# Other loading order and earlier sums of weights in three down stages of a feed-forward kernel

## The chip, the cores and the metric

The kernel runs on one core of a Trainium2 chip. The metric is the device time of one execution in microseconds (us), as a median of runs. A change of under 0.2% (4.9 us here) counts as no change.

## What is computed

The program is two transformer blocks on 256 rows of width 2048, in float32. Only the second feed-forward matters here:

```python
h = rms_norm(x, norm_mlp_pre[l])
u = jnp.square(jax.nn.relu(h @ w_up[l]))          # 256 x 8192
x = x + rms_norm(u @ w_down[l], norm_mlp_post[l])  # w_down: 8192 x 2048
```

A product in full precision is made of three TensorE products in the type fp32r. Each operand is split into a high part (rounded to fp32r) and a low part (the rest); the products are high x high, high x low and low x high.

## The kernel before

**Passes and stages.** The 8192 hidden columns are done in four passes of 2048. A pass is an up stage of 32 steps and a down stage. The down stages of passes 0, 1 and 2 are the full ones that the title speaks of (`DOWN2_STEPS`, 44 steps, numbered 0 to 43 here); the last pass has another list (`LAST_DOWN2`), and the first feed-forward has a third (`DOWN1_STEPS`). A step multiplies by one 256 x 512 piece of weights.

**Plain steps and sevens.** The down product is cut into column blocks b (0 to 3, 512 columns each) and into eighths j of the 2048 rows of weights that a pass uses (0 to 7, 256 rows each). A plain step (b, j) has 12 matmuls. For some pairs of column blocks and groups of rows, four blocks in a 2 x 2 arrangement are multiplied with seven products instead of eight, as in Strassen's method. Such a seven is the steps (pair, group, k), k from 0 to 6, with 6 matmuls each. Products k = 0, 1, 2 take weights as they are loaded. Products k = 3, 4, 5, 6 take sums of weights (sum 0, 1, 2, 3), which VectorE makes by subtraction at L1808. The order of a full down stage begins: steps 0 to 3 plain (0,4) (0,5) (1,4) (1,5); steps 4 to 10 the seven (0,0); steps 11 and 12 plain (0,6) (0,7); steps 13 to 19 the seven (0,1); steps 20 to 23 plain (1,6) (1,7) (2,4) (2,5). Then two more sevens follow, at steps 24 to 30 and 35 to 41.

**The split of a step.** Before TensorE can do step n, ScalarE writes the high part of its weights to `wh` (L908), and then VectorE writes the low part to `wl` (L1464), four slots each. I call them the high part and the low part of n. Both engines work in program order and are three steps ahead: in the program's place s (the s-th turn of the loop, called `ahead(s)`) they split the weights of step s+3. The high part of n waits until TensorE has finished step n-4, whose slot it takes, and until the load has landed. The low part counts `lo_done` up by one, and TensorE's step waits for that count.

**Sums.** `weight_sums` is called after `ahead(s)` and the other work of place s. `sums_begin` says at which place sum 0 is made; the others follow one place apart. Sum 3 takes the buffer of sum 0, so it waits for the low part of product k = 3. For the seven (0,0) the places are 1, 2, 3 and 4, for the seven (0,1) 11, 12, 13 and 14.

**Loads.** Weights come in loads of 1 MB (512 rows of weights by 512 columns, two steps' worth) into four `raw` slots. SyncE's queue issues them in the order of `DOWN2_LOADS`, whose entries are (b, group of rows); the load number u takes slot u mod 4. In front of each issue the queue waits until the load four places earlier is used up:

```python
def ff2_load(u, w, k, col):
    sp.wait_ge(lo_done, load_done(u - RAW_SLOTS))
    sp.dma_start(raw[u % RAW_SLOTS][:], w[:, k:k + 4, col:col + COLS]).then_inc(raw_in[u % RAW_SLOTS], 16)
```

`load_done` gives the count of low parts after which a load's slot is free. For a load that feeds only plain steps this is the low part of its second step: load (0,2) feeds steps 0 and 1, load (1,2) feeds steps 2 and 3, load (0,3) feeds steps 11 and 12. For the two loads of a seven it is the low part of product k = 4 (k = 5 in the seven (0,1)). By then all four sums have been made; for the loads (0,0) and (1,0) this is step 8's low part, made at place 5.

**VectorE's other work around the change.** In the up stages VectorE also adds, squares and splits the hidden values (L2143, L2147, L2165), and in passes 1 and 2 it folds the products of the last pass into the rows (`combine`, L1830 and L1852).

Of the kernel before, what the change touches and what calls it, by code (L numbers as in the profile page):

```python
# [66 lines left out]
def seven(pair, group):  # L67
    return [(pair, group, k) for k in range(7)]
# [17 lines left out]
for _n in range(2):  # L86
# [4 lines left out]

DOWN2_STEPS = [(0, 4), (0, 5), (1, 4), (1, 5)] + seven(0, 0) + [(0, 6), (0, 7)] + seven(0, 1) + [(1, 6), (1, 7)]
DOWN2_STEPS += [(2, 4), (2, 5)] + seven(1, 0) + [(2, 6), (2, 7), (3, 4), (3, 5)] + seven(1, 1) + [(3, 6), (3, 7)]
DOWN2_LOADS = [(0, 2), (1, 2), (0, 0), (1, 0), (0, 3), (0, 1), (1, 1), (1, 3),
               (2, 2), (2, 0), (3, 0), (2, 3), (3, 2), (2, 1), (3, 1), (3, 3)]

LAST_DOWN2 = [(0, 2), (0, 3), (0, 4), (0, 5), (1, 2), (1, 3)] + seven(0, 0)
# [8 lines left out]
for _p in range(UP2_PASSES):  # L106
# [7 lines left out]
DOWNS = [(S_DOWN1[p], L_DOWN1[p], DOWN1_STEPS, DOWN1_LOADS) for p in range(2)]  # L114
DOWNS += [(S_DOWN2[p], LOADS_BEFORE + 32 * p + 16, DOWN2_STEPS, DOWN2_LOADS) for p in range(UP2_PASSES - 1)]
DOWNS += [(S_DOWN2[-1], LOADS_BEFORE + 32 * (UP2_PASSES - 1) + 16, LAST_DOWN2, LAST_LOADS2)]
SEVENS = [(s0 + n, step[0], step[1]) for s0, _, steps, _ in DOWNS for n, step in enumerate(steps)
          if len(step) == 3 and step[2] == 0]


def sums_begin(steps, pair, group):

    late = steps is DOWN2_STEPS and (pair, group) == (0, 1)
    return steps.index((pair, group, 0)) - (2 if late else 3)


def load_of(step):
# [22 lines left out]
def load_done(u):  # L150

    for s0, first, steps, loads in DOWNS:
        if first <= u < first + len(loads):
            b, group = loads[u - first]
            if (b // 2, group, 0) in steps:
                return s0 + sums_begin(steps, b // 2, group) + 8
            return s0 + steps.index((b, 2 * group + 1)) + 1
    if u >= LOADS_BEFORE:
        p, r = divmod(u - LOADS_BEFORE, 32)
        return S_UP2[p] + 2 * r + 2  # L160
    part = max(p for p in range(3) if p == 0 or u >= L_UP1[p])
    return (S_UP1[part] if part else 0) + 2 * (u - (L_UP1[part] if part else 0)) + 2
# [135 lines left out]
def build(nc, a, out, scratch, scratch_cols, scratch_scales):  # L298
# [6 lines left out]
    def at(name, shape, kb, dt=F32):  # L305
        return nc.alloc_sbuf_tensor_at(name, shape, dt, offset=int(base + kb * KB))
# [50 lines left out]
    w_sum = [at(f"w_sum{i}", [P, 2, COLS], kb) for i, kb in enumerate((192, 196, 201))]  # L357
# [170 lines left out]
    def sums_before(q):  # L528

        return 4 * sum(q >= n + 7 for n, _, _ in SEVENS)  # L530
# [22 lines left out]
    def _(sp):  # L553
# [3 lines left out]
        def weight_load(u, i, src):  # L557

            if u >= RAW_SLOTS:
                sp.wait_ge(lo_done, load_done(u - RAW_SLOTS) + 8 * i)  # L560
            sp.dma_start(raw[u % RAW_SLOTS][:], src).then_inc(raw_in[u % RAW_SLOTS], 16)
# [201 lines left out]
# [4 lines that stand above are left out]
# [688 lines left out]
    def _(dve):  # L1455
# [337 lines left out]
        def weight_sum(down, pair, group, n, w_sum):  # L1793

            s0, first_load, steps, loads = DOWNS[down]
            u = first_load + loads.index((2 * pair, group))
            for v in (u, u + 1):
                dve.wait_ge(raw_in[v % RAW_SLOTS], 16 * (v // RAW_SLOTS + 1))
            (b11, b21), (b12, b22) = ([raw[v % RAW_SLOTS][:, 2 * k:2 * k + 2, :] for k in range(2)] for v in (u, u + 1))
            q = s0 + steps.index((pair, group, 0))  # L1800
            made = sums_before(q)
            if n == 2:
                dve.wait_ge(sem["sum_ok"], made + 1)
            if n == 3:
                dve.wait_ge(sem["sum_ok"], made + 3)
                dve.wait_ge(lo_done, q + 4)
            plus, minus = ((b12, b11), (b22, b12), (b22, w_sum[0][:]), (b21, w_sum[2][:]))[n]
            dve.tensor_tensor(w_sum[n % 3][:], plus, minus, ALU.subtract).then_inc(sem["sum_ok"], 1)  # L1808

        def weight_sums(down, s, w_sum):  # L1810

            s0, _, steps, _ = DOWNS[down]
            for n7, step in enumerate(steps):
                if len(step) == 3 and step[2] == 0:
                    n = s - sums_begin(steps, step[0], step[1])
                    if 0 <= n < 4:
                        weight_sum(down, step[0], step[1], n, w_sum)

        def combine(p, pair, k, to_x=True):

            shared, rows_to = (shared1, x_rows) if to_x else (shared2, y_rows)
            (p1, p5), (p6, p7) = ([shared[pair][h][:, c, :] for c in range(2)] for h in range(2))
            (x11, x12), (x21, x22) = ([rows_to[:, t, (2 * pair + b) * COLS:(2 * pair + b + 1) * COLS]
                                       for b in range(2)] for t in range(NT))

            def put(dst, src, t):

                if to_x:
                    return dve.tensor_tensor(dst, src, dst, ALU.add)
                return dve.scalar_tensor_tensor(dst, src, rstd_sq[:, t:t + 1], dst, ALU.mult, ALU.add)  # L1830

            if k == 0:
                dve.wait_ge(sem["shared_out"], 2 * p + pair + 1 if to_x else folds(p, pair))
                if to_x:
                    dve.wait_ge(sem["rows_added"], 16 * (4 * p + 2 * pair + 2))
                elif p:
                    dve.wait_ge(sem["rows_added"], 16 * added(p, 2 * pair + 1))
                else:
                    dve.wait_ge(row_free, FREE + R_DOWN2[0] + 2 * pair + 2)
                put(x11, p1, 0)  # L1840
            if k == 1:
                chain.link(dve.tensor_tensor(p6, p6, p1, ALU.add))
            if k == 2:
                chain.link(dve.tensor_tensor(p7, p7, p6, ALU.add))
            if k == 3:
                put(x21, p7, 1)
            if k == 4:
                chain.link(dve.tensor_tensor(p7, p7, p5, ALU.add))
            if k == 5:
                put(x22, p7, 1)  # L1850
            if k == 6:
                chain.link(dve.tensor_tensor(p5, p5, p6, ALU.add))  # L1852
            if k == 7:
                put(x12, p5, 0).then_inc(sem["combined"], 1)
# [346 lines left out]
        for p in range(UP2_PASSES):  # L2201
            for r in range(S_UP2[p + 1] - S_UP2[p] if p + 1 < UP2_PASSES else N_STEPS - S_UP2[p]):
# [13 lines left out]
                n = r - 32  # L2216
# [53 lines left out]
    def _(pe):  # L2270
# [151 lines left out]
        def head_stage(j, k, last):  # L2422
# [50 lines left out]
            if j == 3 and k - 1 >= first[0]:  # L2473
                n = k - 1
                kind, h, x, _, _, (vb, vc) = heads[n]
                if outs_before(n):
                    pe.wait_ge(sem["at_osb"], outs_before(n))
                acc = psum[:, O_BANK, 0:SEQ]
                if n < N1:
                    v, count = values(n)  # L2480
                    pe.wait_ge(sem["at_vlo"], count)
                    pe.wait_ge(sem["at_ptlo"], n + 1)
                    for kt in range(NT):
                        p_h, p_l = prob_hi[n % 2][:, kt, :], prob_lo[n % 2][:, kt, :]
                        pe.matmul(acc, v[:, 0, kt, :], p_h, start=kt == 0, stop=False)
                        pe.matmul(acc, v[:, 0, kt, :], p_l, start=False, stop=False)
                        ins = pe.matmul(acc, v[:, 1, kt, :], p_h, start=False, stop=kt == 1)
                    ins.then_inc(sem["at_o"], 1)
                    return
                pe.wait_ge(sem["at_ptsb"], n + 1)  # L2490
                if kind == "slc":
                    pe.matmul(acc, cmp_v[:, h % 4, h // 4, :], cmp_pt[:, h // 4, :], start=True, stop=False)
                for kt in range(NT):
                    q0 = P * kt
                    ins = pe.matmul(acc[:, q0:SEQ], x[:, vb, kt, vc:vc + HD], prob_t[n % 2][:, kt, q0:SEQ],
                                    start=False, stop=kind != "slc" and kt == 1)
                ins.then_inc(sem["at_o"], 1)
# [495 lines left out]
```

## Time and profile before

| | |
|---|---|
| median of 3 runs | 2460.39 us (2460.31 to 2460.43) |
| profiled execution, its own time | 2460.36 us |
| its span, first to last instruction | 2458.6 us |
| TensorE busy | 2446.9 us |
| VectorE busy | 1729.2 us |
| ScalarE busy | 1321.1 us |
| mean over 16 DMA engines | 196 GB/s |

The profiled execution lies 0.03 us under the median and 1.8 us over its span, so a difference in the span can be added to the median as it stands. All times inside the kernel count from the start of the span. A matmul is shown with its full duration, of which the next one overlaps a part; what counts is the distance between starts.

### The profile page before, as it was taken

To read this page: it belongs to the slowest core of one execution; us is meant where nothing else is said; L and a number is where in the kernel's file an instruction comes from. 1 tells how busy PE (TensorE), PEld (TensorE's weight loads), DVE (VectorE), ACT (ScalarE), POOL (GpSimd) and SP (SyncE) were. 2 spreads that over 40 slices of the span, in tenths; PEclk is the share of its full clock that TensorE was granted. 3 is DMA by queue.
4 is the path that set the end of the run, shared out by engine and by line. 5 is a ranking of instruction groups with operands and counts; after the bars stand their busy time and mean duration, and the time that the engine had idled before them with its cause. 6 is when DMAs were issued, how large, how long until landed. Compare 5 with 4: busy or idle time off the path is not lost.

```text
span 2458.6 us, 31658 instructions
## 1 busy us (share of the span) xinstructions
PE 2446.9 (100%) x12392; PEld 2073.4 (84%) x12392; DVE 1729.2 (70%) x2080; ACT 1321.1 (54%) x1690; POOL 67.3 (3%) x91
## 2 busy tenths in 40 slices
PE   9999999999999999999999999999999999999998
PEld 7888888888888888888888788888888888888887
DVE  5756767655678777787875457755668779788676
ACT  6444556445555655565555445444646546556453
POOL 0100100000000000000000000000000000000000
PEclk9999999999999999999999999999999999999999
DMA  9655565655555765567557565555564656756763
GB/s 328 207 192 172 164 173 170 224 187 188 190 188 171 245 200 188 188 205 235 182 199 248 157 206 167 163 171 173 171 196 175 228 189 205 222 168 234 218 211 128
DMA packets 255910, 480.84 MB, mean 196 GB/s; under 512 B 23296, under 2 KB 26752, under 8 KB 255152
## 3 DMA queue, kind: packets, MB, share of 16 engines
q1 hardware_dynamic: 251296, 470.85, 57.4%
q0 software_dynamic: 4352, 8.39, 1.9%
q8 instruction: 74, 1.21, 0.2%
q14 instruction: 44, 0.36, 0.0%
q10 hardware_dynamic: 144, 0.03, 0.0%
HBM read 468.71 MB, written 2.13 MB: 192 GB/s over the span
## 4 chain that ended last, share of the span: by engine, by line
PE 96%; DVE 3%; issue 1%; ACT 0%; DVEq 0%; POOLq 0%; POOL 0%; ACTq 0%
PE psum L2376 21%; PE psum L2285 14%; PE psum L2287 14%; PE psum L2286 14%; PE psum L2384 11%; PE psum L2601 3%; PE psum L2603 3%; PE psum L2602 3%; PE psum L2620 2%; PE psum L2622 2%; PE psum L2621 2%; PE psum L2341 1%; DVE wl L1464 1%; PE psum L2346 1%; DVE w_sum L1808 1%
## 5 line engine op out<-in xcount | busy, mean ns | idle before, releaser
L1464 DVE TENSOR_TENSOR wl<-raw,wh 128x1024 fp32r<-128x1024 f32 x833 | 1014.2, 1225 | 647.8 <-ACT wh L908 641.8
L908 ACT ACTIVATE wh<-raw 128x1024 fp32r<-128x1024 f32 x833 | 873.9, 1058 | 774.4 <-PE psum L2287 319.3
L2285 PE MATMUL psum<-wh,ha 128*128 128x512 f32 x1248 | 499.5, 400 | 0.1
L2287 PE MATMUL psum<-wh,ha 128*128 128x512 f32 x1248 | 487.1, 390 | 0.0
L2286 PE MATMUL psum<-wl,ha 128*128 128x512 f32 x1248 | 486.4, 390 | 0.0
L2376 PE MATMUL psum<-ha,wh 128*128 128x512 f32 x1344 | 313.1, 390 | 0.0
L2376 PEld LDWEIGHTS psum<-ha,wh 128*128 128x128 f32 x1344 | 249.7, 188 | 50.1
L2287 PEld LDWEIGHTS psum<-wh,ha 128*128 128x128 f32 x1248 | 234.2, 188 | 50.8
L2285 PEld LDWEIGHTS psum<-wh,ha 128*128 128x128 f32 x1248 | 234.7, 188 | 47.7 <-issue 2.7
L2286 PEld LDWEIGHTS psum<-wl,ha 128*128 128x128 f32 x1248 | 235.0, 188 | 44.7
L2376 PE MATMUL psum<-hb,wh 128*128 128x512 f32 x896 | 209.1, 390 | 0.0
L2376 PEld LDWEIGHTS psum<-hb,wh 128*128 128x128 f32 x896 | 166.4, 188 | 33.4
L2384 PEld LDWEIGHTS psum<-ha,wl 128*128 128x128 f32 x1344 | 166.8, 192 | 3.3
L2384 PE MATMUL psum<-ha,wl 128*128 128x256 f32 x1344 | 167.8, 283 | 0.0
L2384 PEld LDWEIGHTS psum<-hb,wl 128*128 128x128 f32 x896 | 111.2, 192 | 2.2
L2384 PE MATMUL psum<-hb,wl 128*128 128x256 f32 x896 | 111.9, 283 | 0.0
L908 ACT ACTIVATE wh<-w_sum 128x1024 fp32r<-128x1024 f32 x76 | 80.7, 1062 | 50.6 <-PE psum L2603 28.6
L2601 PE MATMUL psum<-wh,ha 128*128 128x512 f32 x240 | 93.6, 390 | 0.7 <-DVE wl L1464 0.7
L1464 DVE TENSOR_TENSOR wl<-w_sum,wh 128x1024 fp32r<-128x1024 f32 x76 | 90.1, 1220 | 4.7 <-ACT wh L908 4.6
L2603 PE MATMUL psum<-wh,ha 128*128 128x512 f32 x240 | 93.4, 389 | 0.0
L2602 PE MATMUL psum<-wl,ha 128*128 128x512 f32 x240 | 93.4, 389 | 0.0
L2285 PE MATMUL psum<-wh,hb 128*128 128x512 f32 x224 | 87.8, 392 | 0.0
(337 smaller groups left out, 2843.6 us busy)
## 6 DMA issues: line engine op xcount, KB each, us to landing
raw<-in_w_up SPq DMA_DIRECT2D x152, 1024.0 KB, 5.1
raw<-in_w_in SPq DMA_DIRECT2D x116, 1024.0 KB, 5.1
raw<-in_w_down SPq DMA_DIRECT2D x108, 1024.0 KB, 5.1
raw<-in_w_out SPq DMA_DIRECT2D x32, 1024.0 KB, 5.0
raw<-in_w_branch_a SPq DMA_DIRECT2D x8, 1024.0 KB, 5.0
raw<-in_w_branch_b SPq DMA_DIRECT2D x8, 1024.0 KB, 4.9
x_rows<-conv POOLq DMA_DIRECT2D x8, 512.0 KB, 6.7
raw<-in_w_in SPq DMA_DIRECT2D x5, 512.0 KB, 8.0
```

The lines of the kernel that those rows point to most:

```text
L908: act.activation(wh[q % SPLIT_SLOTS][:], src, ACT.Copy).then_inc(hi_done, 1)
L1464: dve.tensor_tensor(wl[q % SPLIT_SLOTS][:], src, wh[q % SPLIT_SLOTS][:].bitcast(F32), ALU.subtract).then_inc(lo_done, 1)
L2285: pe.matmul(acc, hi, wh[s][:, c, :], start=first and c == 0, stop=False)
L2286: pe.matmul(acc, hi, wl[s][:, c, :], start=False, stop=False)
L2287: ins = pe.matmul(acc, lo, wh[s][:, c, :], start=False, stop=last and c == 1)
L2376: ins = pe.matmul(psum[:, 4 * v + d, :], wh[s][:, c, P * d:P * d + P], both, start=(j, n, c) == (0, 0, 0), stop=(j, n, c) == (6, 1, 1))
L2384: ins = pe.matmul(psum[:, 4 * v + d, 0:SEQ], wl[s][:, c, P * d:P * d + P], src[:, 2 * (j + n) + c, 0, :], start=False, stop=False)
L2601: pe.matmul(acc, hi, wh[w][:, c, :], start=first and c == 0, stop=False)
L2602: pe.matmul(acc, hi, wl[w][:, c, :], start=False, stop=False)
L2603: ins = pe.matmul(acc, lo, wh[w][:, c, :], start=False, stop=last and c == 1)
L2620: pe.matmul(acc, hi, wh[w][:, c, :], start=first and c == 0, stop=False)
L2621: pe.matmul(acc, hi, wl[w][:, c, :], start=False, stop=False)
```

## The change

The order of the first four loads of a full down stage becomes (0,0), (1,0), (0,2), (1,2). Sums 0, 1 and 2 of the seven (0,0) are made at the places -4, -3 and -2, which are turns 28, 29 and 30 of the up stage before. Sum 3 of every seven is made at the place of its product k = 0, which is where it was for all but the seven (0,1), whose sum 3 moves from place 14 to place 13, directly behind sum 2. `load_done` is rewritten, and comes to the same counts as before for every load of every seven, so (0,0) and (1,0) are released by step 8's low part still. Sum 0 has one more wait, for the low parts of the seven before.

```diff
-DOWN2_LOADS = [(0, 2), (1, 2), (0, 0), (1, 0), (0, 3), (0, 1), (1, 1), (1, 3),
+DOWN2_LOADS = [(0, 0), (1, 0), (0, 2), (1, 2), (0, 3), (0, 1), (1, 1), (1, 3),
                (2, 2), (2, 0), (3, 0), (2, 3), (3, 2), (2, 1), (3, 1), (3, 3)]
...
 def sums_begin(steps, pair, group):
 
-    late = steps is DOWN2_STEPS and (pair, group) == (0, 1)
-    return steps.index((pair, group, 0)) - (2 if late else 3)
+    ahead = {(0, 0): 8, (0, 1): 2}.get((pair, group), 3) if steps is DOWN2_STEPS else 3
+    return steps.index((pair, group, 0)) - ahead
...
             if (b // 2, group, 0) in steps:
-                return s0 + sums_begin(steps, b // 2, group) + 8
+                return s0 + max(sums_begin(steps, b // 2, group) + 8, steps.index((b // 2, group, 4)) + 1)
...
             made = sums_before(q)
+            if n == 0 and made:
+                dve.wait_ge(lo_done, [s + 7 for s, _, _ in SEVENS if s < q][-1])
             if n == 2:
...
                     n = s - sums_begin(steps, step[0], step[1])
-                    if 0 <= n < 4:
+                    if 0 <= n < 3:
                         weight_sum(down, step[0], step[1], n, w_sum)
+                    if s == n7:
+                        weight_sum(down, step[0], step[1], 3, w_sum)
```

## Rows read from the trace of the kernel before

**Rows 1.** The page: busy us (share of the span) xinstructions

```profile
PE 2446.9 (100%) x12392; PEld 2073.4 (84%) x12392; DVE 1729.2 (70%) x2080; ACT 1321.1 (54%) x1690; POOL 67.3 (3%) x91
```

**Rows 2.** Waits of TensorE: us in total, times, longest us

```profile
PE psum L2620 <- DVE wl L1464: 1.1, 4, 0.4
PE psum L2601 <- DVE wl L1464: 0.7, 3, 0.2
```

**Rows 3.** Timeline of TensorE, pass 0's down stage: start, us, line

```profile
1869.64 0.39 PE L2622 MATMUL psum<-wh,ha 128*128 128x512 f32 x1
1870.27 0.47 PE L2601 MATMUL psum<-wh,ha 128*128 128x512 f32 x1 [0.24 <-DVE wl L1464]
...
1875.81 0.39 PE L2620 MATMUL psum<-wh,ha 128*128 128x512 f32 x1
...
1882.98 0.50 PE L2620 MATMUL psum<-wh,a_hi 128*128 128x512 f32 x1 [0.21 <-DVE wl L1464]
...
1885.88 0.39 PE L2601 MATMUL psum<-wh,ha 128*128 128x512 f32 x1
```

**Rows 4.** Timeline of VectorE, the same stage

```profile
1861.87 1.22 DVE L1464 TENSOR_TENSOR wl<-w_sum,wh 128x1024 fp32r<-128x1024 f32 x1
1863.22 1.22 DVE L1808 TENSOR_TENSOR w_sum<-raw,w_sum 128x1024 f32<-128x1024 f32 x1
1864.37 3.48 DVE L1464 TENSOR_TENSOR wl<-w_sum,wh 128x1024 fp32r<-128x1024 f32 x3
...
1868.91 4.62 DVE L1464 TENSOR_TENSOR wl<-raw,wh 128x1024 fp32r<-128x1024 f32 x4
...
1877.16 1.23 DVE L1464 TENSOR_TENSOR wl<-w_sum,wh 128x1024 fp32r<-128x1024 f32 x1 [0.23 <-ACT wh L908]
1878.30 1.22 DVE L1808 TENSOR_TENSOR w_sum<-raw,w_sum 128x1024 f32<-128x1024 f32 x1
1879.44 1.22 DVE L1464 TENSOR_TENSOR wl<-w_sum,wh 128x1024 fp32r<-128x1024 f32 x1
...
1881.71 2.44 DVE L1464 TENSOR_TENSOR wl<-w_sum,wh 128x1024 fp32r<-128x1024 f32 x2
```

**Rows 5.** Timeline of VectorE, last turns of two up stages

```profile
1844.21 2.36 DVE L1464 TENSOR_TENSOR wl<-raw,wh 128x1024 fp32r<-128x1024 f32 x2 [2.14 <-ACT wh L908]
...
2015.84 1.23 DVE L1464 TENSOR_TENSOR wl<-raw,wh 128x1024 fp32r<-128x1024 f32 x1 [2.07 <-ACT wh L908]
```

**Rows 6.** Timeline of ScalarE, pass 0's down stage

```profile
1860.53 1.06 ACT L908 ACTIVATE wh<-w_sum 128x1024 fp32r<-128x1024 f32 x1 [0.71 <-PE psum L2603]
...
1865.97 1.06 ACT L908 ACTIVATE wh<-raw 128x1024 fp32r<-128x1024 f32 x1 [0.30 <-PE psum L2622]
```

**Rows 7.** Timeline of SyncE's queue, pass 0's down stage

```profile
1846.60 5.76 SPq L766 DMA_DIRECT2D raw<-in_w_down  x2
```

**Rows 8.** The tile raw, 1865 to 1867 us: issues, then landing

```profile
L766 SPq DMA_DIRECT2D raw<-in_w_down x2: 368/438/507, 1865.6 to 1866.0; - x2
...
DMA to landing us min/median/max: 5.1/6.2/7.2
```

**Rows 9.** The line L766, all loads of the second feed-forward

```profile
DMA to landing us min/median/max: 4.8/5.2/8.9
```

**Rows 10.** Timeline of TensorE at the kernel's start and end

```profile
1.18 4.64 PE L2504 MATMUL psum<-warm 128*128 128x256 f32 x10 [1.18 <-DVE warm L1627]
5.92 0.74 PE L2285 MATMUL psum<-wh,ha 128*128 128x512 f32 x1
...
6.97 0.39 PE L2285 MATMUL psum<-wh,ha 128*128 128x512 f32 x1
...
2450.48 0.39 PE L2303 MATMUL psum<-wh,ha 128*128 128x512 f32 x1
```

**Rows 11.** Windows at the end: busy by engine, then granted clock

```profile
2450.00:2453.80 3.80, 0.87 (x4) 0.38 (x2) 2.97 (x6) 0.72 (x2) 0.55 (x1) 1.00 0.68 276
2453.80:2458.60 4.80, 0.00 (x0) 0.00 (x0) 2.27 (x4) 0.00 (x0) 0.00 (x0) 0.51 0.57 219
```

## The prediction, made before the changed kernel ran

> **What bounds the kernel now.** I read the page's busy times first. TensorE is busy for 2446.9 of 2458.6 us [rows 1], so nearly every wait of it shows in the end, and it can win back very little. The waits of TensorE come next: in the second feed-forward they are waits for VectorE's low parts, four times in a seven and three times in a plain step, 1.8 us in all [rows 2]. The timelines show where. Three pauses lie ahead of step 11, one in each full down stage, and three ahead of step 18.
>
> The true price is read from distances between starts. In a steady stretch a matmul starts 0.2275 us after the last one: a step of a seven takes 1.365 us, a plain step 2.73 us. Ahead of step 11 the distance is 1870.27 - 1869.64 = 0.63 us instead of 0.23 [rows 3], 0.40 lost. From step 13 to step 20 it is 1885.88 - 1875.81 = 10.07 us where seven steps should take 9.56: 0.51 lost. The first matmuls behind the pause ahead of step 11 also come late: steps 11 and 12 take 1875.81 - 1870.27 = 5.54 instead of 5.46. That makes about 1.0 us a stage, 3.0 us in three. This is all that the change can win, 0.12%.
>
> Why VectorE is late: it starts one operation 1.14 us behind the last. In a seven with its sums it has two for each 1.365 us of TensorE. The timeline shows it without a pause from step 7's low part at 1861.87 over sum 3, the low parts of steps 8, 9 and 10 (one row), the hidden values' low part, to step 11's low part at 1868.91, which ends at 1870.13 [rows 4]. TensorE starts step 11 at 1870.27, 0.14 later.
>
> **The change, part by part.** First the sums 0, 1 and 2 of (0,0). They go to the last three turns but one of the up stage. There VectorE idles for 2.14 us ahead of a pair of low parts in pass 0, and for 2.07 us at the same place in pass 1, where its folds are in the way [rows 5]. Three sums want 3 x 1.14 = 3.4 us. What is pushed back are low parts that TensorE wants more than 3 us later, so I cost this at nothing. If the cover were gone, it would cost up to 3.4 us a stage; I don't expect that, as each plain step gives VectorE 2.73 us for one low part.
>
> What it wins: step 7's high part runs 1860.53 + 1.06 = 1861.59 [rows 6], and its low part can start at 1861.62 instead of 1861.87, as sum 2 no longer stands ahead of it. That is 0.25 us. From there the chain is as before, since sum 3 stays: sum 3 at +1.35 (1863.22 - 1861.87), step 8's low part at +1.15 more and done 1.22 later, so at 1865.34 instead of 1865.59 [rows 4].
>
> **Second, the loads.** The first two loads of the stage are now (0,0) and (1,0), and they keep their slots until step 8's low part. Load (0,3) is the fifth and wants the slot of the first. Before, that was the slot of (0,2), and (0,3) was issued at 1846.60 [rows 7], 19 us ahead of its use. Now it can't be issued ahead of 1865.34, and behind it in SyncE's queue stand (0,1), (1,1) and (1,3). Before, the loads (1,1) and (1,3) were the ones that waited for this: issued at 1865.6 and 1866.0, landed after 5.1 us and, the second, after 7.2 [rows 8]. So of two in a row the second lands 0.4 + 7.2 - 5.1 = 2.5 us behind the first and does not delay it.
>
> Load (0,3) feeds the high part of step 11, which started at 1865.97 [rows 6]. Now:
>
> - issue 1865.35, landing 5.1 later, 1870.45
> - high part from 1870.50 (0.05 is my allowance, within 0 to 0.3) to 1871.56
> - low part from 1871.59 to 1872.81
> - TensorE's step 11 0.14 later, at 1872.95
>
> Before, it was 1870.27: 2.7 us later a stage, with the gain from the sums already in it. It can't be made up, as TensorE has no other slack. The pause itself is 1872.95 - 1869.64 - 0.23 = 3.1 us. The bounds: all landings of the second feed-forward lie between 4.8 and 8.9 us, with a median of 5.2 [rows 9]. The longest ones hold loads that stood behind another, which this one does not, so I keep 4.8 to 5.6: 2.4 to 3.2 us a stage. A stray long landing of 7 us would add 2.
>
> The loads behind it: (0,1) lands at 1873.0, and step 13, which is the first to use it, starts at 1878.5. Load (1,1) at 1875.5 is there when sum 0 of (0,1) comes up, at about 1876.4 behind two late low parts. Load (1,3) at 1878.1 serves step 20. None of them stops TensorE, and VectorE is back in step before 16's low part.
>
> **Third, sum 3 of (0,1) at place 13.** Ahead of it the timeline has the low part of step 16 at 1877.16, sum 2 at 1878.30, the low part of step 17 at 1879.44, sum 3, and the low parts of steps 18 and 19 from 1881.71 [rows 4]. Now sum 3 stands ahead of step 17's low part. It must also wait for the end of sum 2, and this case has a row for it: sum 3 of (0,0), behind a low part that it waits for, starts 1.35 us later and not 1.14. Counted from step 13's start at 1875.81: step 16's low part at +1.35 (set by ScalarE and not by the sums), sum 2 at +2.49, sum 3 at +3.84, step 17's low part at +4.99, done at +6.21. TensorE wants it at 4 x 1.365 = +5.46, and starts at about +6.3. The pause moves from step 18 to step 17 and grows. Step 20 then starts at 6.3 + 3 x 1.365, with 0.1 for the slow first matmuls behind a pause, at +10.5, against +10.07 before: 0.45 us a stage lost. Bounds: nothing, if the wait and the order cost nothing, to 0.6.
>
> The other sevens keep their places; their sum 0 gets a wait for a count that VectorE itself reached long before. No row shows its price. With 18 of them between none and 0.1 us, of which VectorE's idle time hides nearly all, I take none.
>
> **The sum.** 3 x (2.7 + 0.45) = 9.4 us. 2460.4 + 9.4 = 2469.8 us. With the bounds, 3 x (2.4 + 0) = 7.2 to 3 x (3.2 + 0.6) = 11.4, the likeliest case has 2467.6 to 2471.8.
>
> **Rivals.**
>
> *The clock falls in the pause.* At the kernel's end the granted clock is 1.00 until about 2453.8 and then 0.51 over the rest [rows 11]: it fell to the lower level, 1.2 GHz, some 3.0 us after the last matmul, which ran until 2450.48 + 0.39 [rows 10]. My pause in step 11 is 3.1 us. So one, two or all three pauses may end on a slow TensorE. Its price: at the start matmuls ran from 1.18 to about 6.5 before they had full speed, one of them in 0.74 instead of 0.39 us [rows 10]. 5.3 us at half speed lose 2.7 us. One fall gives 2472.5, two 2475.2, three 2477.9. Against it: the pauses are no longer than the one at the end, with full work on both sides.
>
> The Trainium skill, TensorE: Matmul & The Clock Gate, section Why this matters for your kernels, warns of just such idle gaps between bursts of matmuls, and says that the clock goes back to its half rate. By that rule the time would be 2477.9, without it 2469.8; the trace shows the fall only at the end of the program.
>
> *The load is hidden, no change.* Then the change is 3 x 0.45 lost against 3 x 0.25 won: 2461.0 us. It decides at the landing: the high part of step 11 may start as late as 1870.27 - 0.14 - 1.22 - 0.03 - 1.06 = 1867.8, so the load would have to land 2.5 us after its issue. The quickest took 4.8 [rows 9]. Only if I misread which slot it waits for could this come true.
>
> *All stalls go, and it ends on the other side.* If VectorE's chain alone mattered, and both pauses of each stage were gone, the time would be 2460.4 - 3.0 = 2457.4. That is the floor and still within 0.2%. It wants the same early landing, and step 17's low part 0.75 us sooner than I find it.
>
> **Chances.** Load late, clock holds: 0.71. Clock falls at least once: 0.24. Load hidden: 0.04. All stalls gone: 0.01. The range reaches from 2467.4, the low bound of the first, to 2475.5, which takes in one or two falls; it leaves out three falls, the hidden load and a tail. Faster by over 0.2% would be under 2455.5, and no case gives it: 0.01. Within 0.2%: 0.04. Slower by over 0.2%, over 2465.3: 0.95.
>
> **What would show it.** In the changed profile, step 11 of each full stage starts some 3 us behind step 10's last matmul, and the wait for it is put down to `wl` (VectorE), whose own wait is for ScalarE, whose own is for the load. The queue's issues stand four in a row at the end of step 8's low part. Three sums stand in the last turns of the up stage, and VectorE's idle time there is less. Step 17, not 18, has the second pause. The granted clock is 1.00 throughout, or has spells of the lower level behind the pauses. I am wrong if load (0,3) is issued before step 8's low part, or if the landing takes well under 4.8 us; and wrong in size if the clock falls or the landing is held up by the three loads behind it.

## The result and the profile after

The changed kernel takes 2472.73 us (median of 6 runs, 2472.14 to 2475.12). The kernel before takes 2460.41 us in the same comparison. The ratio is 1.0051, 95% interval 1.0042 to 1.0061: 12.3 us slower, which is more than the 0.2% that counts as a change. The profiled execution took 2473.22 us with a span of 2471.5. Three executions of the later comparisons (two of the kernel before, at 2599.82 and 3421.72 us, and one of the version with a fourth buffer, at 3294.64) ran in a slower state of the core and are left out of what follows.

TensorE's waits, after (us in total, times, longest), which answer to [rows 2]:

```profile
PE psum L2605 <- DVE wl L1464: 9.5, 3, 3.7
PE psum L2624 <- DVE wl L1464: 2.6, 4, 0.7
```

There are again three waits ahead of step 11 and four in sevens. Ahead of step 11 they have grown from 0.7 to 9.5 us. In the sevens they have grown from 1.1 to 2.6: the three of the full stages now stand ahead of step 17 instead of step 18, and the fourth, in the last pass, is 0.44 us in both kernels. The timeline of TensorE shows each, as [rows 3] did; the bracket is its idle time and what ended it:

```profile
1872.38 0.55 PE L2605 MATMUL psum<-wh,ha 128*128 128x512 f32 x1 [2.84 <-DVE wl L1464]
...
1876.80 0.40 PE L2605 MATMUL psum<-wh,ha 128*128 128x512 f32 x1
...
1884.76 0.39 PE L2626 MATMUL psum<-wh,a_lo 128*128 128x512 f32 x1
1885.88 0.50 PE L2624 MATMUL psum<-wh,a_hi 128*128 128x512 f32 x1 [0.73 <-DVE wl L1464]
...
2049.48 0.47 PE L2605 MATMUL psum<-wh,ha 128*128 128x512 f32 x1 [3.66 <-DVE wl L1464]
...
2225.90 0.47 PE L2605 MATMUL psum<-wh,ha 128*128 128x512 f32 x1 [3.02 <-DVE wl L1464]
...
2228.71 0.39 PE L2605 MATMUL psum<-wh,ha 128*128 128x512 f32 x1
```

The first, fifth and sixth lines are the starts of step 11 in passes 0, 1 and 2. The third and fourth are step 16's last matmul and the start of step 17 in pass 0. The second and the last are the starts of step 12 in passes 0 and 2: in pass 2 step 11 takes 2228.71 - 2225.90 = 2.81 us, in pass 0 4.42. The windows say why. Their columns are the stretch, its length, the busy time and instructions of PE, PEld, DVE, ACT and POOL, and then the granted clock, the share of the DMA engines and GB/s:

```profile
1869.60:1872.30 2.70, 0.00 (x0) 0.00 (x0) 1.29 (x2) 2.00 (x2) 0.00 (x0) 1.00 1.05 410
1873.00:1876.00 3.00, 3.00 (x8) 2.35 (x8) 2.77 (x4) 1.52 (x2) 0.00 (x0) 0.50 1.05 408
2050.30:2053.30 3.00, 3.00 (x8) 2.32 (x7) 2.88 (x4) 1.21 (x2) 0.00 (x0) 0.50 1.06 407
2226.00:2229.00 3.00, 3.00 (x14) 2.48 (x15) 2.79 (x3) 2.04 (x3) 0.00 (x0) 1.00 1.05 408
```

In 3 us behind the pause TensorE does 14 matmuls in pass 2, at 2.4 GHz, and 8 in passes 0 and 1, at 1.2 GHz. The first line is the pause itself: TensorE does nothing and the DMA engines are full.

What holds it up stands in the chain that ended last, in order of time (start, us, what):

```profile
1862.57 1.23 DVE w_sum L1810
1863.80 1.14 DVE wl L1464
1864.94 0.02 issue
1864.96 4.94 DMA raw<-in_w_down
1869.90 0.02 issue
1869.92 1.06 ACT wh L908
1870.99 0.02 issue
1871.01 1.24 DVE wl L1464
1872.25 0.14 issue
1872.38 0.55 PE psum L2605
```

Before, this stretch was VectorE's work alone, one operation behind another [rows 4]. Now it is sum 3, step 8's low part, the load (0,3) issued at its end, the high and the low part of step 11, and TensorE.

Where the 12.9 us of the span went, worked out from starts of matmuls as in the prediction (a step's distance less 0.2272 us a matmul). Passes 0, 1, 2 in this order:

| lost in us | before | after |
|---|---|---|
| ahead of step 11 | 0.40, 0.40, 0.40 | 3.00, 3.82, 3.18 |
| inside step 11 | 0.10, 0.11, 0.08 | 1.69, 1.69, 0.08 |
| ahead of step 17 or 18, and just behind | 0.52, 0.50, 0.52 | 1.02, 1.02, 1.02 |

With 0.06 a stage inside step 8, which went away, the differences come to 13.3 us. The first full stage began 0.4 us earlier in this execution than in the one before (1848.98 against 1849.39), and 13.3 - 0.4 is the difference of the spans. This start is not the same in every execution: in the traces of this document it lies between 1848.98 and 1849.99, and where two profiled executions are compared below, it is named.

### The profile page after: what moved, and what is told of

Same layout as the page of the kernel before. It is cut to its first block, busy times and chain, and to the rows that moved or that the text cites. A ratio compares the mean times of both kernels' runs of the same rounds, so it can differ in the third digit from the quotient of the medians.

```text
span 2471.5 us, 31658 instructions
## 1 busy us (share of the span) xinstructions
PE 2449.5 (99%) x12392; PEld 2075.7 (84%) x12392; DVE 1730.7 (70%) x2080; ACT 1320.9 (53%) x1690; POOL 67.3 (3%) x91
## 4 chain that ended last, share of the span: by engine, by line
PE 96%; DVE 2%; DMA 1%; ACT 0%; issue 0%; DVEq 0%; POOLq 0%; POOL 0%; ACTq 0%
PE psum L2380 21%; PE psum L2289 14%; PE psum L2291 14%; PE psum L2290 14%; PE psum L2388 11%; PE psum L2605 4%; PE psum L2607 4%; PE psum L2606 4%; PE psum L2624 2%; PE psum L2625 2%; PE psum L2626 2%; PE psum L2345 1%; DVE wl L1464 1%; DMA raw<-in_w_down 1%; PE psum L2350 1%; DVE w_sum L1810 1%
```

## The experiments

**The loading order alone** (no early sum, in the kernel before):

```diff
-DOWN2_LOADS = [(0, 2), (1, 2), (0, 0), (1, 0), (0, 3), (0, 1), (1, 1), (1, 3),
+DOWN2_LOADS = [(0, 0), (1, 0), (0, 2), (1, 2), (0, 3), (0, 1), (1, 1), (1, 3),
```

> The kernel before with the new loading order alone: its sums are made where they were. Theory A (load (0,3) now waits for the slot of (0,0)): the whole pause ahead of step 11 is there without any early sum. Step 8's low part is 0.25 us later than in the changed kernel, so the pause is 3.2 to 4.1 us in each stage instead of 0.6, and the time is 2460.4 + 3 x 2.9 = 2469 us, plus 1.6 for each fall of the clock: 2469 to 2474. The pause ahead of step 18 stays at 0.5 lost. Rival B (three more sums in the last up turns crowd VectorE and make its low parts late): without the sums there is no pause, 2460.4.

Measured: 2475.17 us (2473.08 to 2480.0, 4 runs), ratio 1.0065 (1.0048 to 1.0082). Step 11 of pass 0:

```profile
1873.84 0.77 PE L2601 MATMUL psum<-wh,ha 128*128 128x512 f32 x1 [3.20 <-DVE wl L1464]
```

By the starts, 3.36, 3.91 and 3.33 us are lost ahead of step 11, and 0.5 ahead of step 18 and behind. The pause is there in full without one early sum, so rival B falls. The median lies 1.2 us above the expected 2469 to 2474. The profiled execution, at 2473.48, lies inside it and had the lower clock with two of the three pauses. Of the runs at 2476.86 and 2480 there is no trace; why they took so long stays open.

**The early sums alone** (the changed kernel with the old loading order):

```diff
-DOWN2_LOADS = [(0, 0), (1, 0), (0, 2), (1, 2), (0, 3), (0, 1), (1, 1), (1, 3),
+DOWN2_LOADS = [(0, 2), (1, 2), (0, 0), (1, 0), (0, 3), (0, 1), (1, 1), (1, 3),
```

> The changed kernel with the old loading order, so that load (0,3) finds its slot free early again. Theory A: no pause ahead of step 11 beyond 0.2 us; what is left is 3 x 0.5 for sum 3 of (0,1) against some 3 x 0.3 won on step 11, so 2461.0 us, and the clock stays at 1.00. Load (1,0) now lands about 4 us after sum 0 of (0,0) comes up, which pushes back low parts that TensorE wants 1 us later or more; if this is too tight, up to 1 us a stage more. Rival B: the pause stays, 2469 or more.

Measured: 2463.58 us (2463.35 to 2464.11, 10 runs), ratio 1.0013 (1.0003 to 1.0022). The long pause is gone, as theory A said, and the granted clock stays at 1.00 through all three stages. In pass 0 the loss is what was expected: 0.23 ahead of step 11, and 1.0 ahead of step 17 and behind. In passes 1 and 2 step 11 gains nothing (0.41 and 0.42 us are lost ahead of it, as before), and there is a new pause, 0.81 and 1.05 us ahead of step 8. Four lines of three timelines of pass 1, VectorE's, ScalarE's and TensorE's:

```profile
2017.55 1.22 DVE L1810 TENSOR_TENSOR w_sum<-raw,raw 128x1024 f32<-128x1024 f32 x1 [3.91 <-issue]
...
2030.96 1.22 DVE L2151 SCALAR_TENSOR_TENSOR u_act<-u_sum 128x1024 f32<-128x1024 f32 x1
...
2032.21 1.06 ACT L1385 ACTIVATE ha<-u_act 128x1024 fp32r<-128x1024 f32 x1 [1.84 <-DVE u_act L2151]
...
2038.02 0.50 PE L2624 MATMUL psum<-wh,a_hi 128*128 128x512 f32 x1 [0.65 <-DVE wl L1464]
```

VectorE stands 3.91 us in front of sum 0, until the load (1,0), fourth in line, has landed. With the folds of the last pass it does not catch up: the squaring of the hidden values comes at 2030.96, ScalarE waits for it with its queue behind, step 7's high part is late, and with it sum 3 and step 8's low part. My allowance of "up to 1 us a stage more" holds the sum, 2.6 us over the 2461.0 in three stages. So the early sums do need their loads sooner than third and fourth in line. The fault of the change is not that it moved them, but whose slot was left to the next load.

**Sum 3 of (0,1) back at place 14**, all else as changed:

```diff
-                    if s == n7:
+                    if s == n7 + (down >= 2 and steps is DOWN2_STEPS and (step[0], step[1]) == (0, 1)):
```

> The changed kernel with sum 3 of the seven (0,1) back at place 14. Theory A: the distance from step 16 to step 17 falls back to 1.37 us and the one ahead of step 18 is about 1.7 again; 0.5 us less a stage, so 1.5 less than the changed kernel for an equal number of falls of the clock: 2467.7 with none, 2469.3 with one, 2470.9 with two. Rival: the place of sum 3 costs nothing, because VectorE has the same work either way; then as the changed kernel, 2472 to 2475.

Measured: 2473.74 us (2473.5 to 2474.91, 4 runs), ratio 1.0053 (1.0036 to 1.007). By itself this time speaks for the rival, whose range was 2472 to 2475. The rows agree with theory A: the pause is ahead of step 18 again and 0.50 us are lost there and behind, in each stage, instead of 1.02. But the profiled execution, at 2474.91, had the lower clock in all three stages, and in the third for longer: 2.5 us are lost inside step 11 and 0.4 inside step 12. Against the profiled execution of the changed kernel, 2.6 us more are lost inside steps 11 and 12, 0.3 less ahead of step 11, the first full stage begins 0.9 later (1849.87), and sum 3 gives back 1.5: together 1.7 us more, as measured (2474.91 - 2473.22). The next experiment has sum 3 alone, where no long pause stands in the way.

**Sum 3 of (0,1) at place 13**, in the kernel before:

```diff
-                    if 0 <= n < 4:
+                    if 0 <= n < 3:
                         weight_sum(down, step[0], step[1], n, w_sum)
+                    if s == n7:
+                        weight_sum(down, step[0], step[1], 3, w_sum)
```

> The kernel before with one thing of the change: sum 3 of the seven (0,1) at place 13, behind sum 2 and ahead of step 17's low part. Theory A: the pause moves from step 18 to step 17 and 1.02 us are lost there instead of 0.52, in each stage: 2460.4 + 1.5 = 2461.9 us. Rival: the two orders cost the same, 2460.4.

Measured: 2462.03 us (2461.75 to 2462.22, 11 runs), against 2460.41 of the kernel before: 1.6 us more, where 1.5 was expected. The interval of the ratio, 0.9997 to 1.0015, does not exclude 1. But each of the 11 runs lies above the runs of the kernel before (2459.98 to 2460.83), and the rows show the cause. VectorE's timeline, then TensorE's step 17:

```profile
1878.48 1.22 DVE L1808 TENSOR_TENSOR w_sum<-raw,w_sum 128x1024 f32<-128x1024 f32 x1
1879.90 1.23 DVE L1808 TENSOR_TENSOR w_sum<-raw,w_sum 128x1024 f32<-128x1024 f32 x1 [0.20 <-DVE w_sum L1808]
1881.04 3.49 DVE L1464 TENSOR_TENSOR wl<-w_sum,wh 128x1024 fp32r<-128x1024 f32 x3
...
1882.31 0.50 PE L2622 MATMUL psum<-wh,a_hi 128*128 128x512 f32 x1 [0.73 <-DVE wl L1464]
```

Sum 3 starts 1.42 us behind sum 2, for whose end it waits, and step 17's low part stands behind it.

**The loads (0,3) and (0,1) released by sum 3** of the seven (0,0), all else as changed. They are issued one VectorE operation sooner:

```diff
-            sp.wait_ge(lo_done, load_done(u - RAW_SLOTS))
+            p, n = divmod(u - LOADS_BEFORE, 32)
+            if p < UP2_PASSES - 1 and n in (20, 21):
+                sp.wait_ge(sem["sum_ok"], sums_before(S_DOWN2[p]) + 4)
+                sp.wait_ge(lo_done, S_DOWN2[p] + 7)
+            else:
+                sp.wait_ge(lo_done, load_done(u - RAW_SLOTS))
```

> The changed kernel, but the two loads (0,3) and (0,1) wait for sum 3 of (0,0) (and the low part of step 6) and not for the low part of step 8, so they are issued 1.14 us sooner. Theory A: the pause ahead of step 11 shrinks by 1.1 us, from 3.0 to 1.9, in each stage, which is too short for the clock to fall: 2472.7 - 3.4 for the pauses and - 3.2 for two falls, so 2466 us, granted clock 1.00 in between. Rival C (the landing is bound by the four transfers in a row, not by its issue): the pause stays near 3 us and the clock still falls, 2472.

Measured: 2466.76 us (2466.19 to 2469.34, 10 runs), ratio 1.0026 (1.0017 to 1.0036). The pauses are 2.05, 1.96 and 1.98 us by the starts instead of 3.00, 3.82 and 3.18: they follow the issue. Rival C falls. The time is near the expected 2466. But the clock of the profiled execution, the longest of the ten, did not do what I expected. TensorE's step 11 in the three passes, and windows behind it:

```profile
1871.56 0.47 PE L2610 MATMUL psum<-wh,ha 128*128 128x512 f32 x1 [1.89 <-DVE wl L1469]
...
2046.79 0.47 PE L2610 MATMUL psum<-wh,ha 128*128 128x512 f32 x1 [1.80 <-DVE wl L1469]
...
2220.44 0.64 PE L2610 MATMUL psum<-wh,ha 128*128 128x512 f32 x1 [1.82 <-DVE wl L1469]
```

```profile
1873.00:1875.50 2.50, 2.50 (x7) 1.92 (x7) 2.50 (x3) 0.71 (x1) 0.00 (x0) 0.50 1.05 408
2047.00:2050.00 3.00, 3.00 (x14) 2.45 (x14) 2.73 (x3) 2.07 (x3) 0.00 (x0) 1.00 1.05 410
2221.00:2223.50 2.50, 2.50 (x8) 1.92 (x7) 2.29 (x3) 1.55 (x2) 0.00 (x0) 0.50 1.05 408
```

Pauses with 1.89 and 1.82 us of idle time brought the lower clock, and one with 1.80 did not. Less its two falls, at 1.6 us each, this execution would be at 2466.1, and five of the ten lie between 2466.19 and 2466.54. They probably had no fall; no trace shows it.

**Load (0,3) second in line**, behind (0,1), all else as changed:

```diff
-DOWN2_LOADS = [(0, 0), (1, 0), (0, 2), (1, 2), (0, 3), (0, 1), (1, 1), (1, 3),
+DOWN2_LOADS = [(0, 0), (1, 0), (0, 2), (1, 2), (0, 1), (0, 3), (1, 1), (1, 3),
```

The code takes a seven's loads as neighbours, so here the sums of (0,1) are made from the loads (0,1) and (0,3) instead of (0,1) and (1,1). The operations are as many and as long.

> The changed kernel with loads (0,1) and (0,3) exchanged, so that (0,3) is issued second in line. Theory A (a load behind another lands 2.55 us after it): the pause ahead of step 11 is 2.55 us longer, 5.6 to 6.4 us, in each stage, and the clock falls in all three: 2472.7 + 7.7 + 1.6 = 2482 us, or up to 1.5 us less for each fall that begins while TensorE still waits. Rival (TensorE waits for something else than this landing): no change, 2472.

Measured: 2487.69 us (2487.01 to 2488.12, 4 runs), ratio 1.0111 (1.0096 to 1.0127). ScalarE's wait for the load, and TensorE's step 11, in pass 0:

```profile
1873.44 2.95 ACT L908 ACTIVATE wh<-raw 128x1024 fp32r<-128x1024 f32 x3 [7.32 <-DMA raw<-in_w_down]
...
1875.90 0.76 PE L2605 MATMUL psum<-wh,ha 128*128 128x512 f32 x1 [5.50 <-DVE wl L1464]
```

The pauses are 5.66, 6.33 and 5.73 us by the starts, 2.5 to 2.7 longer than in the changed kernel, as theory A said. The lower clock is there in all three stages. Of the 5.7 us above the expected 2482, 3.4 are new pauses: load (2,2) now waits for the slot of (0,1), and about 1.1 us a stage are lost ahead of steps 22 and 28 and just behind. Another 0.9 is the first full stage, which begins at 1849.83 in the profiled execution and at 1848.98 in that of the changed kernel. The lower clock is not in the excess: 1.44, 1.64 and 2.06 us are lost inside step 11, 1.7 more in sum than in the changed kernel, where 1.6 was expected.

**A mended order**, with both loads of the sums among the first three and (0,3) on the slot of (0,2), sum 3 of (0,1) at place 14, and the release by sum 3 for the loads (0,1) and (1,1):

```diff
-DOWN2_LOADS = [(0, 0), (1, 0), (0, 2), (1, 2), (0, 3), (0, 1), (1, 1), (1, 3),
+DOWN2_LOADS = [(0, 2), (0, 0), (1, 0), (1, 2), (0, 3), (0, 1), (1, 1), (1, 3),
...
-                    if s == n7:
+                    if s == n7 + (down >= 2 and steps is DOWN2_STEPS and (step[0], step[1]) == (0, 1)):
```

> A version meant to keep the gain without the loss: order (0,2), (0,0), (1,0), (1,2), so that (0,3) takes the slot of (0,2) and both loads of the sums are there by the last up turns; the loads (0,1) and (1,1) wait for sum 3 instead of the low part of step 8; sum 3 of (0,1) stays at place 14. Theory A: the pause ahead of step 11 is 0.23 + 0.08 lost instead of 0.55, ahead of step 18 as before, so 2460.4 - 0.7 = 2459.7 us, granted clock 1.00. Rival D (a load of the sums that is second or third in line comes too late again, as it did with the early sums alone): VectorE waits in front of sum 0 and the time is 2461 to 2463.

Measured: 2459.69 us (2459.51 to 2460.43, 11 runs), ratio 0.9998 (0.9989 to 1.0007), against 2460.41 before. The median is where theory A put it, 0.7 us down, but by the ratio it is no difference that can be told. Ten of the 11 runs (2459.51 to 2459.89) lie below every run of the kernel before (from 2459.98). TensorE's last matmul of step 10 and the start of step 11 in pass 0:

```profile
1869.52 0.39 PE L2631 MATMUL psum<-wh,ha 128*128 128x512 f32 x1
1869.99 0.47 PE L2610 MATMUL psum<-wh,ha 128*128 128x512 f32 x1
```

So 0.24 us are lost ahead of step 11, in each pass, instead of 0.40. None is lost inside step 8, and 0.50 ahead of step 18 and behind, as before. Rival D falls.

**A fourth buffer for the sums.** All four sums of (0,0) are made in the up stage, their loads are free after step 6's low part, and the sums of (0,1) begin two places earlier. The core of the edit:

```diff
-    ahead = {(0, 0): 8, (0, 1): 2}.get((pair, group), 3) if steps is DOWN2_STEPS else 3
+    ahead = {(0, 0): 8, (0, 1): 4}.get((pair, group), 3) if steps is DOWN2_STEPS else 3
...
+            if steps is DOWN2_STEPS and (b // 2, group) == (0, 0):
+                return s0 + steps.index((0, 0, 2)) + 1
...
-    w_sum = [at(f"w_sum{i}", [P, 2, COLS], kb) for i, kb in enumerate((192, 196, 201))]
+    w_sum = [at(f"w_sum{i}", [P, 2, COLS], kb) for i, kb in enumerate((192, 196, 201, 184))]
...
-                    if s == n7:
+                    first = down >= 2 and steps is DOWN2_STEPS and step[:2] == (0, 0)
+                    if s == (-1 if first else n7):
```

> The changed kernel with a fourth buffer for sums, so that sum 3 of (0,0) is made at place -1 and its loads are released by the low part of step 6 (some 5.3 us sooner); the sums of (0,1) are made at places 9, 10, 11 and 13. Theory A: load (0,3) is issued about 1859.7 and lands 1864.8, ahead of its use at 1866.0; VectorE has one operation for each of TensorE's steps from 7 to 10, so no pause is left ahead of step 11, 17 or 18. All of the 3.0 us: 2457.4 to 2458.0 us. Rival E (the time of VectorE is short over the whole stage, and moving sums only moves the pause): within 0.5 us of 2460.4.

Measured: 2458.67 us (median of 10 runs, 2458.16 to 2458.98), ratio 0.9992 (0.9983 to 1.0002), where 2457.4 to 2458.0 was expected. No pause is left ahead of step 11. Ahead of step 17 remain 0.31, 0.54 and 0.24 us and 0.13 behind each: 1.5 us in all, half of the 3.0 that could be won. Rival E, within 0.5 us of 2460.4, falls.

**The same with sum 3 of (0,1) at place 14**, behind step 17's low part (and its two loads released one low part later):

```diff
-                    if s == (-1 if first else n7):
+                    late = down >= 2 and steps is DOWN2_STEPS and step[:2] == (0, 1)
+                    if s == (-1 if first else n7 + late):
```

> The version with four buffers, with sum 3 of the seven (0,1) back at place 14 and the release of its two loads one low part later. Before this move 0.25 to 0.55 us a stage were left, ahead of step 17. Theory A: sum 3 stood ahead of step 17's low part for nothing; behind it there is room, since VectorE is not behind at place 13. No pause is left, 3 x 0.3 us less, 2457.8 us. Rival E (the pause only moves to step 18, as VectorE's time is short): 2458.7, as with sum 3 at place 13.

Measured: 2457.95 us (2457.64 to 2458.24, 11 runs), ratio 0.9990 (0.9980 to 0.9999). TensorE's waits, and VectorE in pass 0 from step 7's low part on:

```profile
PE psum L2637 <- DVE wl L1472: 0.6, 2, 0.4
```

```profile
1861.93 5.31 DVE L1472 TENSOR_TENSOR wl<-w_sum,wh 128x1024 fp32r<-128x1024 f32 x4 [1.49 <-ACT wh L916]
1867.15 1.22 DVE L2182 TENSOR_TENSOR ha<-u_act,ha 128x1024 fp32r<-128x1024 f32 x1
1868.29 2.35 DVE L1472 TENSOR_TENSOR wl<-raw,wh 128x1024 fp32r<-128x1024 f32 x2
1870.71 1.23 DVE L1821 TENSOR_TENSOR w_sum<-raw,raw 128x1024 f32<-128x1024 f32 x1
```

Steps 7 to 10 get their low parts in a row with no sum between, and sum 0 of (0,1) comes 2.7 us sooner than in the kernel before. Of the two waits, 0.44 us is the one in the last pass, which every kernel here has; the other is what is left ahead of step 18 in pass 1, with 0.33 us lost. This version is 2.5 us below the kernel before (2460.47 in its comparison) and 14.8 below the changed one. Each of its runs lies below each of the kernel before (from 2460.09), but 2.5 us is 0.1%, and by the metric that is no change.

## Why the prediction was right, and where it was not

The direction, the mechanism and the place were right, and 2472.73 lies in the range of 2467.4 to 2475.5. (The low end does not fit the prediction's own sum, which gives 2460.4 + 7.2 = 2467.6.) The likeliest case, 2469.8 with the clock held, is not what happened: 9.4 us were forecast and 12.3 measured. In the profiled execution the load with the early sums makes 8.8 us (8.1 forecast), sum 3 of (0,1) 1.5 (1.35 forecast) and the lower clock 3.2 (none in the likeliest case); 0.2 went away in step 8 and 0.4 at the first stage's start, which leaves the 12.9 of the span. That the time came so well inside the range is in part luck: two falls at the forecast price gave 2475.2, near its upper end, and the price was too high. Step by step:

- **The gain from the early sums.** Step 7's low part was to be set by ScalarE, and step 8's low part to end 0.25 us sooner. After, the first waits for ScalarE (it started at 1861.21, with 1.49 us of idle time ahead of it), and the order alone has pauses 0.36, 0.09 and 0.15 us longer. The mended order, where nothing else is in the way, won 0.7 us in three stages, 0.24 each, and 0.25 was forecast. The early sums were to cost nothing in the up stage, and with the loads first they cost nothing: no step of the up stage or of the first eight lost time. With the loads late (the early sums alone), the same sums cost 0.8 to 1.1 us in a pass with folds.
- **Load (0,3).** Forecast: issue, 5.10 to the landing, high part, low part, step 11, 2.7 us later a stage. Measured: 4.94 in pass 0, and 2.60, 3.42 and 2.78 us more ahead of step 11. The chain of the profile has each link as forecast. In pass 1 the landing took 5.8 us, 0.7 longer than the 5.1 of pass 2 and 0.2 over my bound of 5.6. The order alone, sum 3 at place 14 and (0,3) second in line show the late landing in pass 1 too, the release by sum 3 does not. Two things stand beside it in each of these four traces, and in no other pass of theirs or of the release by sum 3: SyncE's second issue comes 0.70 us behind the first instead of 0.41 to 0.47, and one packet of 8 KB on the DMA queue for instructions runs 4.0 to 4.2 us after the first issue. Whether either is the cause was not tested, so it stays open.
- **Sum 3 of (0,1).** Forecast 0.45 us a stage; the changed profile has 0.50, and alone it cost 1.6 us in three stages. The pause stood ahead of step 17, as forecast.
- **The clock.** This is the step that failed: "the pauses are no longer than the one at the end" was taken as a reason to give a fall 0.24. The fall at the kernel's end came some 3.0 us after the last matmul [rows 10, 11], and I read that as the pause that it takes. Pauses with 1.82 and 1.89 us of idle time brought it too, and 3.02 in pass 2 of the changed kernel did not. By the rows at hand, without a fall the changed kernel would be at about 2470: pass 2, with none, lost 3.2 us more than before, and 3 x 3.2 = 9.6. The price was mis-sized as well: 2.7 us a fall was forecast from the kernel's start, and each fall in the changed kernel cost 4.42 - 2.81 = 1.6 us. It is no fixed price: the longer spell in sum 3 at place 14 cost 2.5 + 0.4 - 0.1 = 2.8. The 1.6 fits the six runs roughly: three at 2472.14 to 2472.24, two at 2473.22 and 2473.41, one at 2475.12, steps of 1.1 and 1.8 us. Only the one at 2473.22 has a trace, with two falls; the count of the others is argued, not shown.

The Trainium skill, TensorE: Matmul & The Clock Gate, section Why this matters for your kernels, was right that such pauses can cost the clock. Its rule was the rival, and by it all three would fall; the traces show two of three in the changed kernel and with the order alone, and all three in sum 3 at place 14 and with (0,3) second in line. The clock also fell behind pauses that are shorter than the gaps which the section warns of, with 1.82 and 1.89 us of idle time in the release by sum 3; there the measurement decides.

The rivals of a hidden load and of all stalls gone fell with the first profile. The floor of 2457.4 that I worked out for the latter was nearly reached by another edit, at 2457.95.

## What to carry to other kernels

With a ring of slots, moving a load to the front is not one edit. It exchanges slots: ask for each later load whose slot it takes now, when that one is released, and whether a landing time fits between the release and the use. Where several operations move together, cost each alone: here the early sums won some 0.24 us a stage, the order lost some twelve times as much, and one sum a single place too early lost twice as much. Hold a pause of TensorE against the clock too, even one of 2 us, and read the price from a step behind it.

## What was not expected of the hardware

The granted clock fell to 0.50 in the middle of otherwise full work, with pauses of 1.82 to 6.17 us of idle time, and not with others of like length: 1.80, 3.02 and 3.17 us had none (the last in pass 2 of the order alone). So no length between 1.82 and 3.17 us told here whether a fall would come. In the changed kernel's pass 0 it came a fraction of a microsecond behind the end of the pause, when TensorE already worked again. Pauses of 0.15 to 0.84 us never brought it in any profile here. Four loads in a row landed 2.6 us apart at about 408 GB/s, and the first was not held up by the three behind it in passes 0 and 2 (4.94 and 5.1 us from issue to landing, against 5.1 before).
